# Order of the 64- and 32-column pieces of the 96-slot experts, and a place for the second rank in the second pass

## What is computed

```
logits = h @ w_router + b_router
top_v, top_i = top_k(logits, 2);  top_w = softmax(top_v)
gates = sum(one_hot(top_i, 8) * top_w)
for e in range(8):
    out = out + gates[e] * ((silu(h @ w_gate[e]) * (h @ w_up[e])) @ w_down[e])
```

## Time and profile before

| | |
|---|---|
| Median of 3 runs | 1790.09 us (1789.62 to 1790.26) |
| Profiled execution, its own time | 1790.85 us |
| Its span | 1789.1 us |
| TensorE busy | 1706.7 us, 95% |
| VectorE, ScalarE busy | 36%, 20% |
| Moved by DMA | 396.18 MB, mean 221 GB/s over the span |
| Mean granted TensorE clock | 0.98 of full |

### The profile page before, as it was taken

One profiled execution on the slowest core, in us unless ns is written; L12 is line 12 of the kernel. 1 busy time (PEld: TensorE's weight loads), 2 busy tenths in 40 slices (PEclk: granted clock), 3 DMA queues, 4 the chain that ended last, 5 costly groups with the idle time before them and its releaser, 6 DMA issues.

```text
span 1789.1 us, 23244 instructions
## 1 busy us (share of the span) xinstructions
PE 1706.7 (95%) x9661; PEld 878.3 (49%) x9661; DVE 645.0 (36%) x1479; ACT 350.6 (20%) x749; POOL 73.5 (4%) x147
## 2 busy tenths in 40 slices
PE   6999999799999999989988899999999999999996
PEld 3655454288888844437866654343223222322232
DVE  5988961755545404155894520000000000000002
ACT  4324550311111100025373320000000000000001
POOL 2110100000000030000110000000000000000000
PEclk9999999899999999989999799999999999999998
DMA  8414542723332152252433099999999999999992
GB/s 306 149 18 159 194 127 94 226 56 95 95 94 80 44 109 64 88 226 94 119 92 100 0 371 376 372 384 409 343 407 392 409 343 404 389 409 331 408 390 91
DMA packets 194984, 396.18 MB, mean 221 GB/s; under 512 B 34339, under 2 KB 104587, under 8 KB 188730
## 3 DMA queue, kind: packets, MB, share of 16 engines
q1 hardware_dynamic: 189504, 391.23, 60.6%
q0 software_dynamic: 4112, 3.34, 1.2%
q10 hardware_dynamic: 1258, 0.07, 0.0%
HBM read 389.36 MB, written 1.05 MB: 218 GB/s over the span
## 4 chain that ended last, share of the span: by engine, by line
PE 91%; DVE 4%; ACT 3%; DMA 2%; issue 1%; ACTq 0%; DVEq 0%; SPq 0%
PE ps L978 88%; PE ps L981 2%; DMA work<-in_w_ada_dram 1%; DVE rstd L1823 1%; DVE aT L1831 0%; DVE work L1840 0%; ACT dg L671 0%; ACT work L662 0%; ACT work L663 0%; DVE hT L1845 0%; DMA work<-in_conv_b_dram 0%; ACT work L778 0%; DVE aT L2057 0%; ACT std L727 0%; ACT aT L735 0%
## 5 line engine op out<-in xcount | busy, mean ns | idle before, releaser
L978 PE MATMUL ps<-ring,work 128*32 128x256 f32 (+4 forms) x3088 | 545.1, 499 | 1.7 <-ACT work L922 1.1
L978 PEld LDWEIGHTS ps<-ring,work 128*64 128x64 f32 (+2 forms) x3088 | 166.9, 128 | 366.8 <-issue 364.0
L978 PE MATMUL ps<-work,ring 128*128 128x512 f32 (+1 forms) x656 | 237.0, 514 | 1.3 <-DVE work L2139 1.3
L978 PE MATMUL ps<-aT,ring 128*128 128x256 f32 (+1 forms) x800 | 235.2, 443 | 2.9 <-ACT aT L735 2.2
L2277 DVE TENSOR_TENSOR work<-work,ps 128x512 f32<-128x512 f32 (+4 forms) x27 | 19.5, 730 | 586.5 <-PE ps L978 586.5
L978 PE MATMUL ps<-aT,work 128*64 128x512 f32 (+4 forms) x1088 | 210.6, 468 | 0.0
L978 PE MATMUL ps<-work 128*64 128x64 f32 (+8 forms) x1984 | 194.8, 298 | 9.7 <-DVE work L2107 5.0
L978 PEld LDWEIGHTS ps<-aT,ring 128*128 128x128 f32 x800 | 152.4, 192 | 72.4 <-issue 54.4
L978 PEld LDWEIGHTS ps<-work,ring 128*128 128x128 f32 x656 | 124.5, 190 | 106.4 <-issue 98.5
L978 PEld LDWEIGHTS ps<-work 128*64 128x64 f32 (+5 forms) x1984 | 143.1, 155 | 52.2 <-issue 38.9
L978 PEld LDWEIGHTS ps<-aT,work 128*64 128x64 f32 (+2 forms) x1088 | 104.0, 147 | 93.8 <-issue 84.4
(11 more groups left out here) (345 smaller groups left out, 1258.3 us busy)
## 6 DMA issues: line engine op xcount, KB each, us to landing
ring<-in_moe_w_down_dram SPq DMA_DIRECT2D x70, 1024.0 KB, 8.5
ring<-in_moe_w_gate_dram SPq DMA_DIRECT2D x50, 1024.0 KB, 8.2
ring<-in_moe_w_up_dram SPq DMA_DIRECT2D x48, 1024.0 KB, 10.4
ring<-in_w_ada_dram SPq DMA_DIRECT2D x23, 2048.0 KB
ring<-in_moe_w_up_dram SPq DMA_DIRECT2D x32, 768.0 KB, 7.8
aT<-in_moe_w_down_dram SPq DMA_DIRECT2D x18, 1024.0 KB, 8.6
ring<-in_moe_w_gate_dram SPq DMA_DIRECT2D x24, 768.0 KB, 7.3
aT<-in_moe_w_up_dram SPq DMA_DIRECT2D x16, 1024.0 KB, 8.1
```

The costliest lines, as they stand in the source:

```text
L978: return pe.matmul(o, lhs, rhs, start=start, stop=stop)
```

## The change

In `project_in`, a 96-slot expert runs the 64-column pieces of two blocks, and behind the second the 32-column pieces of both (`last_slots`), each of which then raises `block_used`. `project_out` does the same; in the 768 chunk, which has three down blocks, the third has its 32-column pieces behind its own 64-column ones. The 128- and 64-slot experts keep their order. All products and their operands stay the same.

For the second pass, `select(1)` adds to the slot of a token of rank 1 whose place is 96 or more behind the first pass' end an offset of `SLOT0[NH] - SLOT0[2]`. Behind `gates(0)`, VectorE computes a second table `who2_i`: where some expert has more left than 128 slots, the first of the 64-slot ranks is given to rank 1's expert. SP uses this table in the second pass and waits for `routed` 2 ahead of it. The sum over `totals` that was kept in `who` goes to `key`, so that `who` survives.

```diff
@@ project_in
+                    def last_slots(n, d):
+                        lhs = [xg[:, 2 * d + j, SLOT0[r] + HP:SLOT0[r + 1]] for j in range(2)]
+                        for j in range(2):
+                            for g in range(w // 256):
+                                last = mm(ps[TP * g:TP * g + TP, bank + 1, 0:256], lhs[j],
+                                          wblock(n)[:, j, 256 * g:256 * g + 256], d + j == 0, 2 * d + j == KC - 1)
+                        last.then_inc(sem("block_used"), 1)
...
-                                if big(i):
-                                    lhs = xg[:, k, SLOT0[r] + HP:SLOT0[r + 1]]
-                                    for g in range(w // 256):
-                                        last = mm(ps[TP * g:TP * g + TP, bank + 1, 0:256], lhs,
-                                                  b[:, j, 256 * g:256 * g + 256], k == 0, k == KC - 1)
-                        last.then_inc(sem("block_used"), 1)
+                        if heavy(i) or not big(i):
+                            last.then_inc(sem("block_used"), 1)
+                        elif d % 2:
+                            last_slots(n - 1, d - 1)
+                            last_slots(n, d)
                         n += 1
                         between(d)
@@ project_out
+                    def last_slots(n, d):
+                        for t in (2 * d, 2 * d + 1):
+                            for g in range(4):
+                                last = mm(ps[TP * g:TP * g + TP, 6, 0:256], hTs[:, i % 2, 4 + t % 2, TP * (t // 2):TP * (t // 2) + TP],
+                                          wblock(n)[:, t % 2, 256 * g:256 * g + 256], c == 0 and t == 0, c == NC - 1 and t == tiles - 1)
+                        last.then_inc(sem("block_used"), 1)
...
-                            if big(i) and not heavy(i):
-                                for g in range(4):
-                                    last = mm(ps[TP * g:TP * g + TP, 6, 0:256], hTs[:, i % 2, 4 + t % 2, TP * (t // 2):TP * (t // 2) + TP],
-                                              b[:, j, 256 * g:256 * g + 256], first, end)
-                        last.then_inc(sem("block_used"), 1)
+                        if heavy(i) or not big(i):
+                            last.then_inc(sem("block_used"), 1)
+                        elif d % 2 or d == blocks - 1:
+                            for e in range(d // 2 * 2, d + 1):
+                                last_slots(n - d + e, e)
@@ select, second pass only
+                    link(tt_(slot_of[:], slot_of[:], late[:], ALU.add))
+                    link(ts_(late[:], rel[:], float(HP + TP), float(SLOT0[NH] - SLOT0[2]), ALU.is_ge, ALU.mult))
+                    link(ts_(key[:], rank[:], 1.0, None, ALU.is_equal))
+                    link(tt_(late[:], late[:], both(key[:]), ALU.mult))
@@ behind gates(0)
+            link(tt_(key[:], key[:], cap[:], ALU.subtract))
+            link(dve.tensor_reduce(far[:, 0:1], key[:], AX_X, ALU.max))
+            link(ts_(far[:, 0:1], far[:, 0:1], float(2 * HP), None, ALU.is_gt))
+            link(tt_(far[:, 1:2], who[:, 1:2], who[:, NH:NH + 1], ALU.subtract))
+            link(stt(who[:, NH:NH + 1], far[:, 1:2], far[:, 0:1], who[:, NH:NH + 1], ALU.mult, ALU.add))
+            dve.tensor_copy(who2_i[:], who[:]).then_inc(sem("routed"), 1)
@@ SP
-            experts(0, ranking())
-            sp.wait_ge(sem("routed"), 1)
+            experts(0, ranking(who_i))
+            sp.wait_ge(sem("routed"), 2)
...
-                experts(1, ranking())
+                experts(1, ranking(who2_i))
```

More of the change, by code:

```diff
@@ L192, in hybrid_backbone @@
         who_i = sb("who_i", [P, NE], I32)
+        who2_i = sb("who2_i", [P, NE], I32)
+        far = sb("far", [P, 2])
         most = sb("most", [P, 1])
@@ L534, in _, with ranking @@
             sp.wait_ge(sem("ranked"), 1)
-            def ranking():
-                return nc.values_load_multi_w_load_instructions(who_i[0:1, 0:NE], engines=[mybir.EngineType.SP],
+            def ranking(by_rank):
+                return nc.values_load_multi_w_load_instructions(by_rank[0:1, 0:NE], engines=[mybir.EngineType.SP],
                                                                 min_val=0, max_val=NE - 1)[1]
-            experts(0, ranking())
-            sp.wait_ge(sem("routed"), 1)
+            experts(0, ranking(who_i))
+            sp.wait_ge(sem("routed"), 2)
             over = sp.value_load(most_i[0:1, 0:1], min_val=0, max_val=S)
             with sp.If(over > 0):
-                experts(1, ranking())
+                experts(1, ranking(who2_i))
             for i in range(2):
@@ L1483, in project_out @@
                         pe.wait_ge(sem("y_ready"), 2 * (p0 + i // 6))
-                    for d in range(w // 256):
+                    tiles, blocks = w // P, w // 256
+                    def last_slots(n, d):
[4 more added lines that the diff above has]
+                        last.then_inc(sem("block_used"), 1)
+                    for d in range(blocks):
                         pe.wait_ge(sem(f"block_in{n % NBUF}"), 16 * (n // NBUF + 1))
@@ L1488, in project_out @@
                             t = 2 * d + j
-                            first, end = c == 0 and t == 0, c == NC - 1 and t == w // P - 1
-                            h, u = divmod(t, w // 256)
+                            first, end = c == 0 and t == 0, c == NC - 1 and t == tiles - 1
+                            h, u = divmod(t, blocks)
                             for g in range(2):
@@ L2238, in _ @@
             dve.wait_ge(sem("ranked"), 1)
-            link(tt_(who[:], totals, cap[:], ALU.subtract))
-            link(dve.tensor_reduce(most[:], who[:], AX_X, ALU.max))
+            link(tt_(key[:], totals, cap[:], ALU.subtract))
+            link(dve.tensor_reduce(most[:], key[:], AX_X, ALU.max))
             link(ts_(most[:], most[:], -float(HP), 0.0, ALU.add, ALU.max))
```

## The result

The changed kernel takes 1758.3 us (median of 4 runs, 1756.58 to 1759.43) against 1789.86 us before: ratio 0.9823, 95% interval 0.9806 to 0.984. That is 31.6 us less; 1759 was forecast.

What follows compares the result with a forecast made beforehand. TensorE's issue pattern was taken as the bound; it would save 44.3 us, but transfers at 402 GB/s would limit the gain to about 31.5 us. From 1790.85 that gave 1759.3, adjusted to 1759 us, range 1745 to 1771.

Steps and rivals of the forecast that it cites:

- The bound before: Expert stage, 96-slot experts: TensorE's own issue pattern sets the time, 180 us a round, never waiting for a block.
- Part 1: 96-slot products: 156 pairs of shape changes removed at 0.29 us each, less 0.9 us; TensorE saves 44.3 us.
- Part 2: Block releases in twos: first of a pair free about 1.4 us later, hidden by stock; otherwise up to 1.4 us a pair.
- stock: Landed expert blocks waiting in the ring of ten: some 14 us of cover, 10 us of the forecast gain.
- Part 3: Block transfers in 96-slot rounds: TensorE would need 419 GB/s, queues hold about 402, so the gain is 31 to 32 us.
- Part 4: VectorE's added operations after the first gates: 1.2 us, hidden in its 35.5 us wait; second pass not run, costing nothing.
- A: Rival on transfers: they keep up at 409 GB/s and the whole 44.3 us saving arrives, 1746 us; chance 0.10.
- C: Rival on 96-slot steps: the 0.29 us belongs to each 32-column group, so nothing is saved, 1790 us; chance 0.05.
- B: Rival on transfers: less efficient; 378 to 391 GB/s gives 1790 to 1772 us (0.05), below 378 slower than before (0.06).
- D: Rival on TensorE's clock: some 13 waits each lose 1.6 us to a lowered clock, 21 us, 1780 us; chance 0.04.

Runs made afterwards that it cites:

- in_turn_paired_release: The kernel before, with blocks of 96-slot experts released in twos and products in the old order: 1790.64 us, ratio 0.9999, stage 717.33 us.
- groups_of_four: The changed kernel with the 32-column pieces behind four blocks instead of two: 1761.48 us, ratio 0.9833 against the kernel before, stage 686.30 us.
- the eleventh buffer: The changed kernel with a ring of eleven block buffers instead of ten: 1756.22 us, ratio 0.9805 against the kernel before, stage 682.35 us.
- old_half_loads: The kernel before, loading only half of each expert block's columns after the ring's first filling: 1790.57 us, ratio 1.0001, stage 717.34 us.

## Why the prediction was right, point by point

The forecast of 1759 us (1758.6 before rounding) was met to a microsecond by the median of 1758.3. That closeness is in part luck: the start of the stage moves by up to 3.4 us between profiles and the part behind it by 1.7. The stage itself is the better measure: 31.3 to 32.3 us less were forecast, 32.87 measured.

**The bound before** was TensorE's issue alone: halving the transfers changed the stage by 0.01 us.

**Part 1, 0.29 us per pair of shape changes.** Right. Measured 43.64 us for the whole against 44.3, 30.09 us for 105 pairs (0.287 each), 5.45 us for four steps. The 0.215 us for 32-column passes back to back, which no row of this stage had shown, held, at the lower of the two bounds. What a pair's 0.29 us consist of, no run separates. By the Trainium skill, "TensorEngine Tiling (Array Packing)", section "Key Properties", changing the tiling mode drains the engine, while moving to another tile in the same mode doesn't. The runs agree with that as far as they can show it: 105 changes fewer each way are worth 30.09 us, and among the 32-column tiles of one run no such cost appears (0.215 a pass).

**Part 2, releases in twos.** Right where there is stock: in_turn_paired_release, 717.33 us. What they cost once the stock is gone ("up to 1.4 us" a pair) has no run of its own. groups_of_four, which holds four blocks, has 4.5 us more of waits and a stage 1.8 us longer than the changed kernel; how much of the waits comes from holding and how much from a faster TensorE stays open.

**Part 3, where the stall goes.** Right in place, and in size to 2 us. The sum had the products end at 1733 to 1734 with 503.5 us of transfers at 402 GB/s; they ended at 1733.5 with 403. It had 44.3 - 31.5 = 12.8 us of waits; the halved loads give 10.8. Of the 2.0 between them, 0.7 are TensorE's saving, which was smaller (43.64), and 1.0 is the stage's start, which was later while the products ended where they were forecast. The split of the gain into 22 us of transfers that no longer pause and 10 of stock wasn't measured; the eleventh buffer's 2.1 us fit the stock. Had the forecast stopped at the 44 us of part 1, it would have been 12 us off.

**Part 4, VectorE and the second pass.** Right: 1790.93 us with them alone, beside 1790.69. `select` gets four new operations and not three; in these runs the second pass isn't run, so nothing here prices them.

**Rivals.** A (all of it arrives) and C (nothing is saved) are excluded by the two kernels with halved loads; A is what happens there. B (less efficient transfers) didn't come: issues in pairs ran at 403. D (the clock falls at waits) didn't come either: 1.00 over 1227 to 1730 with all 15 waits inside, each at most 1.1 us.

But the row on which D's price rested is less firm than it looked. The wait of 1.67 us ahead of the last spreading stands in all 14 profiles. Here it is before and after the change, and below it the stretch behind it in the changed kernel:

```profile
1766.93 1.23 PE L978 MATMUL ps<-work 64*128 64x512 f32 x2 [1.67 <-DVE work L2260]
```

```profile
1735.09 1.12 PE L980 MATMUL ps<-work 64*128 64x512 f32 x2 [1.67 <-DVE work L2292]
```

```profile
1735.00:1740.00 5.00, 4.91 (x21) 3.04 (x22) 1.41 (x3) 1.22 (x2) 0.00 (x0) 1.00 0.02 5
```

In the kernel before, the clock fell behind it (0.60 over 1768 to 1772 us, 0.50 over the first 2 of these); in the changed kernel it stayed at 1.00. It fell in seven of the 14 profiles and stayed in the other seven, old_half_loads among them, which issues the same products as the kernel before. That is the 1.7 us by which the part behind the stage varies. So a wait of that length doesn't decide by itself whether the clock falls, and one row of it is no price. The Trainium skill, "TensorE: Matmul & The Clock Gate", section "HAM oscillation — how this bites in real kernels", tells of slices whose products take less time than the wait for the next one, so that each starts cold. In the changed kernel no wait for a block is over 1.1 us, and the products between two of them take 1.9 us or more. So the forecast took that case for this one too readily, and no run tests it.

## What to carry to other kernels

Price a change of array shape from two rows, a run of one shape and an alternation of two, and count how many a reordering removes; here they were 43.6 of the 717 us of the stage. Then ask, per round and not per span, what rate the faster engine will demand: here 419 GB/s where no window showed over 410, and that comparison decided a quarter of TensorE's saving (10.8 of 43.6 us). And compare the stage that was changed rather than the whole, when what lies ahead of it and behind it moves by as much as the effect. Grouping pays until the next limit: the first halving of the shape changes brought 30 of 33 us, the second 3, the third took 2 back.

## What the runs showed of the hardware

- Stage lengths of equal TensorE work repeat to 0.01 us (717.33, 717.34, 717.33, 717.34 in four profiles of four kernels), while the start of the stage moves by up to 3.4 us and the part behind it by 1.7.
- Behind one and the same wait of 1.67 us the granted clock fell to about half in seven profiles and stayed at full in seven; fifteen waits of 0.2 to 1.1 us within dense work left it at 1.00.
- Rows of half the length move less per busy time: 204 GB/s at a share of 0.63 and 191 at 0.62, which would be 324 and 308 at full share, against 403 at 1.02 for whole rows.
